# A hybrid encoder kernel: the recurrent mixer's triangular solve in blocks of 8 with Horner steps

## The reference

```python
def rwkv_scan(r, w, k, v, kk, b, reverse):
    def step(state, inp):
        r_t, w_t, k_t, v_t, kk_t, b_t = inp
        sa = jnp.einsum('bhvk,bhk->bhv', state, -kk_t)
        state = (state * w_t[:, :, None, :] + sa[..., None] * b_t[:, :, None, :]
                 + v_t[..., None] * k_t[:, :, None, :])
        return state, jnp.einsum('bhvk,bhk->bhv', state, r_t)
...
    for d in range(2):
        w_log = -jax.nn.softplus(-(w0[d] + jnp.tanh(z @ w1[d]) @ w2[d])) - 0.5
        decay = heads(jnp.exp(-jnp.exp(w_log.astype(f32))))
        a = jax.nn.sigmoid(a0[d] + (z @ a1[d]) @ a2[d])
        kd = heads(k * (1.0 + (a - 1.0) * k_a))
        ys.append(rwkv_scan(rh, decay, kd, vh, kk, kk * heads(a), reverse=(d == 1)))
```

## Time and profile before

| | |
|---|---|
| time, median of 3 runs | 3765.77 us (3765.65 to 3765.84) |
| profiled execution | 3762.42 us, span 3760.6 us |
| mean granted clock of PE | 0.994 of 2.4 GHz |
| PE matmul busy | 3675.8 us, 98% |
| PE weight loads busy | 3401.5 us, 90% |
| DVE busy | 2378.3 us, 63% |
| ACT busy | 424.9 us, 11% |
| recurrent mixer's groups, first layer | 347.3 to 541.0 us |

### The profile page before, as it was taken

One profiled execution on the slowest core, in us unless ns is written; L12 is line 12 of the kernel. 1 busy time (PEld: TensorE's weight loads), 2 busy tenths in 40 slices (PEclk: granted clock), 3 DMA queues, 4 the chain that ended last, 5 costly groups with the idle time before them and its releaser, 6 DMA issues. The chain is left out here.

```text
span 3760.6 us, 63506 instructions
## 1 busy us (share of the span) xinstructions
PE 3675.8 (98%) x26848; PEld 3401.5 (90%) x26848; DVE 2378.3 (63%) x4235; ACT 424.9 (11%) x1010; POOL 1169.8 (31%) x926
## 2 busy tenths in 40 slices
PE   7999999999999999999989999999999999999998
PEld 6778885999999999999977888859999999999998
DVE  7986853894688654444389867539946885444442
ACT  1014211100111000000010232111101110000000
POOL 3610000033333355554245100001333334554552
PEclk9999999999999999999999999999999999999999
DMA  5440113599999999999653401146999999999995
GB/s 167 143 136 23 35 58 118 203 398 409 392 388 405 378 364 362 361 358 371 227 158 123 133 29 35 53 127 226 393 413 385 394 408 380 373 369 359 353 364 205
DMA packets 312536, 994.17 MB, mean 264 GB/s; under 512 B 59341, under 2 KB 170317, under 8 KB 231053
## 3 DMA queue, kind: packets, MB, share of 16 engines
q0 software_dynamic: 118944, 587.71, 40.5%
q1 hardware_dynamic: 193312, 402.41, 29.1%
HBM read 1071.38 MB, written 2.10 MB: 285 GB/s over the span
## 5 line engine op out<-in xcount | busy, mean ns | idle before, releaser
L1840 PE MATMUL bank<-ycT,ex_tile 128*128 128x160 f32 x8192 | 1130.5, 299 | 0.0
L1840 PEld LDWEIGHTS bank<-ycT,ex_tile 128*128 128x128 f32 x8192 | 1115.8, 190 | 7.0 <-issue 6.7
L1913 PEld LDWEIGHTS bank<-ex_W,ex_tile 128*128 128x128 f32 x8192 | 1113.3, 190 | 6.8 <-issue 6.7
L1913 PE MATMUL bank<-ex_W,ex_tile 128*128 128x160 f32 x8192 | 1116.6, 299 | 0.0
L1779 POOL DMA_INDIRECT ex_row<-in_peer_u,ex_rows x244 | 256.8, 1052 | 1529.3 <-DVE ex_rows L2073 1062.1
L2115 DVE CUSTOM_DVE_ANT_0 ex_row<-ex_row,ex_h_wide 128x2048 f32<-128x2048 f32 x192 | 439.1, 2290 | 355.3 <-DMA ex_row<-in_peer_u,ex_rows 353.9
L2121 DVE SCALAR_TENSOR_TENSOR ex_sums<-ex_row,ex_weight,ex_sums 128x2048 f32<-128x2048 f32 x186 | 437.3, 2351 | 349.7 <-DMA ex_row<-in_peer_v,ex_rows 349.4
L1790 POOL DMA_INDIRECT ex_tile<-in_peer_v,ex_wanted x256 | 314.1, 1227 | 486.6 <-PE bank L1913 435.7
L459 PE MATMUL pj_bank<-pj_hT,pj_piece 128*128 128x256 f32 x2048 | 454.6, 382 | 4.4 <-DVE pj_hT L813 4.4
L459 PEld LDWEIGHTS pj_bank<-pj_hT,pj_piece 128*128 128x128 f32 x2048 | 387.3, 190 | 70.2 <-issue 13.7
L1779 POOL DMA_INDIRECT ex_row<-in_peer_v,ex_rows x128 | 125.6, 981 | 247.7 <-DVE ex_sums L2121 187.8
(11 more groups left out here) (395 smaller groups left out, 3460.9 us busy)
## 6 DMA issues: line engine op xcount, KB each, us to landing
ex_tile<-in_peer_uT SPq DMA_DIRECT2D x256, 1024.0 KB, 8.1
pj_piece<-in_w_in SPq DMA_DIRECT2D x32, 2048.0 KB, 8.5
arena<-in_w_out SPq DMA_DIRECT2D x20, 1024.0 KB, 5.1
query_w<-in_peer_w_query SPq DMA_DIRECT2D x16, 1024.0 KB, 6.0
rw_low_rank<-in_w_out SPq DMA_DIRECT2D x12, 512.0 KB, 4.1
ex_row<-in_peer_u,ex_rows POOLq DMA_INDIRECT x314, 9.6
ex_row<-in_peer_v,ex_rows POOLq DMA_INDIRECT x256, 8.8
ex_tile<-in_peer_v,ex_wanted POOLq DMA_INDIRECT x256, 7.9
```

Of the source, the lines that this page charges most:

```text
L1840: mm = mmul(o, ring[:, j % SLOTS, k * P:k * P + P], hT[k // 4][:, k % 4, 0:DENSE], start=(k == 0), stop=(k == KT - 1))
L1913: mm = mmul(bank[:, at_, lo:lo + DENSE], ring[:, i % SLOTS, m * P:m * P + P], W[:, j, :], start=(j == 0 and m % 3 == 0), stop=(j == TILES ...
```

## The change

The block size of the solve goes from 16 to 8. In blocks of 8, N^8 is zero, so W = (I + N + N^2)(I + N^3 + N^6), which is built in two Horner steps: W3 = I + N + N^2 (`w3`), W6 = W3 + N^3 W3 (`h1`), W = W3 + N^3 W6 (`h2`). The part outside the blocks now has four block rows in a chunk, so that (W No)^4 is zero: with M = W No and X0 = W R, R = X0 + M (X0 + M (X0 + M X0)), three Horner steps (`y1`, `y2`, `y3`), each a product and an add on DVE. Nine products a direction stand where eleven stood. The filler in the solve is cut in two halves. `prepare_decays` is split: the scans stay early, and the reciprocal with the four small copies becomes `prepare_inverse`, which follows the last add of the solve. Token shifts and the key square are spread between the steps.

```diff
-    mats["N4T"], mats["N4"], mats["N8"] = mats["NT"], mats["N"], mats["N2T"]
-    Yo = mats["N2"]
+    mats["W6"], mats["W"], mats["MT"] = mats["NT"], mats["N"], mats["N2T"]
+    mats["X0"], mats["X1"], mats["X2"] = mats["Aak"], mats["N3"], mats["W3"]
...
                 for d in range(2):
                     dve(f"nn{d}")
-                    product(d, 2 + 2 * d, mats["N"], mats["NT"])
-                    ev(product(d, 3 + 2 * d, mats["NT"], mats["N"]))
+                    ev(product(d, 2 + 2 * d, mats["N"], mats["NT"]))
                 act("trA")
                 turn("trB", 7, lambda d, b: BTc[:, d, b * P:b * P + P])
                 for d in range(2):
-                    act(f"sq2{d}")
-                    product(d, 2 * d, mats["N2"], mats["N2T"])
-                    ev(product(d, 2 * d + 1, mats["N2T"], mats["N2"]))
+                    act(f"n2{d}")
+                    ev(product(d, 3 + 2 * d, mats["N2T"], mats["N"]))
...
                 for d in range(2):
-                    ev(product(d, 4 + d, mats["N2"], mats["W"]))
-                fill(3 * i)
+                    act(f"n3{d}")
+                    dve(f"w3{d}")
+                    ev(product(d, 2 + 2 * d, mats["N3"], mats["W3"]))
+                fill(3 * i, [0])
                 for d in range(2):
-                    act(f"sq4{d}")
-                    dve(f"w2{d}")
-                    ev(product(d, d, mats["N4"], mats["W"]))
+                    dve(f"h1{d}")
+                    ev(product(d, 3 + 2 * d, mats["N3"], mats["W6"]))
...
+                fill(3 * i, [1])
                 for d in range(2):
-                    ev(product(d, 2 + d, mats["N4T"], mats["N4"]))
+                    dve(f"h2{d}")
+                    ev(product(d, d, mats["W"], R))
+                    ev(product(d, 2 + 2 * d, mats["No"], mats["W"]))
                 for d in range(2):
-                    act(f"sq8{d}")
-                    dve(f"w4{d}")
-                    ev(product(d, 4 + d, mats["N8"], mats["W"]))
+                    act(f"m{d}")
+                    ev(product(d, 3 + 2 * d, mats["MT"], mats["X0"]))
                 for d in range(2):
-                    dve(f"w8{d}")
-                    ev(product(d, d, mats["W"], R))
+                    dve(f"y1{d}")
+                    ev(product(d, d, mats["MT"], mats["X1"]))
                 for d in range(2):
-                    act(f"x{d}")
-                    ev(product(d, 2 + d, mats["NTo"], R))
-                for d in range(2):
-                    act(f"no{d}")
-                    ev(product(d, 4 + d, mats["W"], Yo))
+                    dve(f"y2{d}")
+                    ev(product(d, 2 + 2 * d, mats["MT"], mats["X2"]))
...
                         masked(d, b0, 1, "Rb", "m32" + w + "i", wait=False)
-                        masked(d, b0, 0, "NT", "m16" + w, wait=False)
-                        masked(d, b0, 0, "NTo", "mX" + w, dve_ev)
+                        masked(d, b0, 0, "NT", "m8" + w, dve_ev)
...
-                    do(V.tensor_tensor(eb(mats["N"], d), src, m4("m16" + "LU"[d]), ALU.mult), dve_ev, wait=(d == 1))
+                    do(V.tensor_tensor(eb(mats["N"], d), src, m4("m8" + "LU"[d]), ALU.mult), wait=False)
+                    do(V.tensor_tensor(eb(mats["No"], d), src, m4("mX" + "LU"[d]), ALU.mult), dve_ev, wait=(d == 1))
...
-                grow("w2")
-                grow("w4")
-                grow("w8")
+                    shift(sv[:], 2, i + 1)
+                add("h2", (3, 5), mats["W"], mats["W3"])
                 if i % 2:
                     add_unit((1, 4)[i // 2])
                 if more:
                     prepare_3(i + 1)
-                for d in range(2):
-                    pe(f"z{d}")
-                    do(V.tensor_tensor(jk(R, d), bank[:, 4 + d, :], jk(R, d), ALU.add), dve_ev, wait=False)
+                add("y1", (3, 5), mats["X1"], mats["X0"])
+                add("y2", (0, 1), mats["X2"], mats["X0"])
+                add("y3", (2, 4), R, mats["X0"])
                 if more:
+                    prepare_inverse(nc, do, first)
                     prepare_pairs(nc, do, first, i + 1)
```

More of the change, by code:

```diff
@@ L279, in prepare_decays @@
 def prepare_decays(nc, do, first, i):
[L281 to L282 removed]
+    V, dec, D1, Pc = nc.vector, decay(first, i), first["D1"], first["Pc"]
     for d in range(2):
@@ L1145, in head_sums, with fill @@
                 mmul(bank[:, 7, 0:SEQ], c("heads"), kq[:], start=True, stop=True).then_inc(kq_mm, 1)
-            def fill(m):
+            def fill(m, blocks=range(TB)):
                 u, br = divmod(m, 2)
[L1150 to L1153, removed]
+                if blocks[0] == 0:
+                    pe.wait_ge(chunk_in[m % 4], 16 * (m // 4 + 1))
+                    if m >= 2 and br == 0:
+                        pe.wait_ge(unit_added, u)
+                for b in blocks:
                     for k in range(GT):
@@ L1369, in _ @@
                 for d in range(2):
-                    pe(f"sq2{d}")
-                    do(A.copy(jk(mats["N2T"], d), bank[:, 2 + 2 * d, :]), wait=False)
-                    do(A.copy(jk(mats["N2"], d), bank[:, 3 + 2 * d, :]), act_ev, wait=False)
+                    pe(f"n2{d}")
+                    do(A.copy(jk(mats["N2T"], d), bank[:, 2 + 2 * d, :]), act_ev, wait=False)
                 pe("trB")
@@ L1375, in _ @@
                 for d in range(2):
-                    pe(f"sq4{d}")
-                    do(A.copy(jk(mats["N4T"], d), bank[:, 2 * d, :]), wait=False)
-                    do(A.copy(jk(mats["N4"], d), bank[:, 2 * d + 1, :]), act_ev, wait=False)
+                    pe(f"n3{d}")
+                    do(A.copy(jk(mats["N3"], d), bank[:, 3 + 2 * d, :]), act_ev, wait=False)
                 pe("trK")
@@ L1382, in _ @@
                     kk_root(i + 1)
-                for name, dst, b0 in (("sq8", mats["N8"], 2), ("x", R, 0), ("no", Yo, 2)):
-                    for d in range(2):
-                        pe(f"{name}{d}")
-                        do(A.copy(jk(dst, d), bank[:, b0 + d, :]), act_ev, wait=False)
+                for d in range(2):
+                    pe(f"x{d}")
+                    do(A.copy(jk(mats["X0"], d), bank[:, d, :]), act_ev, wait=False)
+                    pe(f"m{d}")
+                    do(A.copy(jk(mats["MT"], d), bank[:, 2 + 2 * d, :]), act_ev, wait=False)
                 for d in range(2):
@@ L1464, in _, with add @@
                                        pend[:, d, :].unsqueeze(2).to_broadcast([P, NCH, RH]), ALU.mult), wait=(d == 1))
-                def grow(name):
+                def add(name, b0, to, plus):
                     for d in range(2):
                         pe(f"{name}{d}")
-                        do(V.tensor_tensor(jk(mats["W"], d), bank[:, (0 if name == "w4" else 4) + d, :],
-                                           jk(mats["W"], d), ALU.add), dve_ev, wait=False)
+                        do(V.tensor_tensor(jk(to, d), bank[:, b0[d], :], jk(plus, d), ALU.add), dve_ev, wait=False)
                 more = i < GT - 1
-                if not more:
+                for d in range(2):
+                    dve.wait_ge(act_ev, at(ACT_EV, i, f"n2{d}"))
+                    do(V.tensor_tensor(jk(mats["W3"], d), jk(mats["N2T"], d), jk(mats["W3"], d), ALU.add), dve_ev, wait=False)
+                if more:
+                    shift(sr[:], 0, i + 1)
+                    shift(sk[:], 1, i + 1)
+                else:
                     scale_branch(nc, do, col, first, ycT, 2)
                     dve.sem_inc(branch_ready, 1)
+                add("h1", (2, 4), mats["W6"], mats["W3"])
                 if more:
-                    prepare_1(i + 1)
+                    do(V.scalar_tensor_tensor(kq[:], sk[:], col("k_k", i + 1), sk[:], ALU.mult, ALU.mult))
+                    do(V.tensor_scalar(kq[:], kq[:], col("k_k", i + 1), None, ALU.mult), kq_ready)
                     prepare_decays(nc, do, first, i + 1)
-                grow("w2")
-                grow("w4")
-                grow("w8")
+                    shift(sv[:], 2, i + 1)
+                add("h2", (3, 5), mats["W"], mats["W3"])
                 if i % 2:
```

31 lines of the change are left out of this document (16 added, 15 removed).

## The result

The changed kernel takes 3769.84 us (median of 20 runs, 3765.22 to 3773.93), the kernel before 3765.52 us beside it (20 runs, 3757.86 to 3771.12). The ratio is 1.0013 [1.0007, 1.0019]: 4.3 us more, inside 0.2% and inside the stated range, but on the other side of where the forecast of 3757 stood. Nine products for eleven bought nothing as the change stands.

The account below looks back on a forecast made before the run. PE bounds the kernel, DVE close behind, and DVE becomes the bound in groups 0 to 2. Queues -9.6, old half clock -4, new falls +5 give -8.6 us: median 3757, range 3746 to 3771 (own case 3750 to 3763).

Parts of the forecast that it names:

- The wait: Before direction 1's G/H products in groups 0 to 2: PE waits about 4 us, where it was 0.3.
- Four more DVE operations: DVE's queue in each group: ten operations removed, fourteen added, costing 2.6 us more.
- Groups 1 and 2 unchanged by the queues: Groups 1 and 2 of a layer: DVE sets the pace, 43.7 against 44.2 us, length unchanged within 0.5 us.
- Group 3, -4.0: Group 3 of a layer, preparing no next group: PE sets the pace, saved products count in full, -4.0 us.
- Group 0, -0.8 a layer: Group 0 of a layer: products behind the masks come 1.2 us sooner, DVE takes part back, -0.8 us.
- the old falls, -4: Half clock behind group 0's mask waits, both layers: 8.2 us lost in all, half counted as gained, -4 us.
- the price of a fall: Half clock behind each of the six new PE waits: 0.8 us each, +5 us in all.
- The signs: Profile signs: PE wait about 4 us, DVE idle under 3, mask to G add 43 to 44.5, group 3 near 42.4.
- The third: Rival: falls over dense work cost about 2 us each, old ones half kept; -1.6 us, 3764; 27%.
- The fourth: Rival: slower, six falls of 4.5 us each and mask waits keep theirs; +17 us, 3783; 8%.
- The first: Rival: PE stays the bound everywhere, all 28.6 us are gained; 3737 us; 5%.
- The second: Rival: waits come without clock falls, the mask waits' half clock goes too; -17.8 us, 3748; 15%.

Follow-up runs that it names:

- the move alone: Kernel before with only the reciprocal and four small copies put behind the last add of the solve, all eleven products kept: 3801.58 us, ratio 1.0095.
- the kernel whose waits are filled: Changed kernel plus eight unused 256-column matmuls in PE's wait before direction 1's G/H products, groups 0 to 2: 3751.32 us, ratio 0.9970.

## Why the prediction missed

- **The wait came as forecast.** DVE's tail grew, PE's saved 3.6 us a group came back as one wait ahead of direction 1's G/H products in groups 0 to 2: forecast about 4 us, measured 4.02 six times. Its cause is the move (the move alone gives 4.20).
- **Four more DVE operations, 2.6 us.** Right: group 1 has 2.56 us more of DVE (41.86 for 39.30).
- **Groups 1 and 2 unchanged by the queues.** With the clock kept +0.1 and -0.1 us. Right.
- **Group 3, -4.0.** With the clock kept 46.10 for 50.14, -4.0. Right.
- **Group 0, -0.8 a layer, and the old falls, -4.** Together -5.6 forecast for the two layers; measured -3.3 and -4.7, -8.0, since the mask waits' half clock was gone in both layers of the profile. At 3.1 us for 6.8 us of half clock nearly all of this is the clock. The price was sized right there, and that both falls were gone is in part luck of this execution: over all profiles the old solve's two mask waits have half clock behind them in six of six cases, the new solve's one wait in four of fourteen. Profiles of other kernels with the same code at this place have it in one layer and not in the other (43.93 and 47.12 us for group 0 in one profile).
- **The step that failed: the price of a fall, "0.8 each, six of them: +5".** The falls came behind all six waits, as forecast, and cost 2.4 us each, 14.2, by the kernel whose waits are filled. With 14.2 in place of 5 the forecast's own sum is +0.6 us where it was -8.6: no gain. I had taken the first layer's 6.8 us and written that "more than half lies over idle and small products, costs about 1.5", then cut it again for shorter ones. No fall was shorter, and PE is busy 5.93 of the 6.8 us. The rows to see it were at hand: behind the wait come the end of the G/H products and the BH pairs, 2.00 us at full clock, and the first mask of DVE's queue waits for just these pairs. That queue sets the pace of the group, so what the pairs lose is lost. The half clock also began 0.5 to 0.9 us after work came back, not in the wait, so the wait couldn't absorb it.
- **The signs.** Between first mask and G add of group 1 are 45.56 us, with 5.0 of DVE idle, where 43 to 44.5 and under 3 were named; with the clock kept they are 44.31 and 3.7, of which 2.7 are waits and the rest small gaps. DVE's busy time there, forecast as 40.6, was 40.57. Group 3 lost 1.9 us, not 4.0. These misses too are the clock's, but for 0.7 us by which the estimate of some 2 for DVE's waits was too small.
- **The rivals.** The third, "about 2 us each", is the one that came closest: -1.6 by its sum, with 3764 us (the median lies 5.8 above that). With the measured parts: group queues and old falls -15.7, falls +14.2, together -1.5 for the eight groups. The fourth needed 2.9 us a fall, which no fall reached. The first is out. The second describes the kernel whose waits are filled: 14.4 us under before by the medians, where it had 17.8.
- **Still open.** The medians differ by +4.3 us, the groups by -1.5. In the profiles the two state loops have 2.1 us more and the rest of the program 2.2, both in code that is the same. Of the 2.1, 1.8 are one idle time of PE in each loop, in which it waits for nothing that the profile shows (ahead of line 1326, formerly 1320): 0.96 and 0.94 us before, 1.87 and 1.85 after. The kernel with the filled wait took 78.36 and 78.07 us for these loops, as before. I have no cause for it. The changed kernel's profile was also the fastest of its 20 runs, 4.6 us under their median, with a granted clock of 0.991, and others had down to 0.988. Other kernels' profiles have half clock in two more places, at the mask wait of group 0 (3.1 us) and in a state loop (80.5 to 81.7 us for some 78.2, in one of the two loops of five kernels). That the changed kernel's longer runs have these is likely and not shown; the runs of one kernel spread over 9 to 13 us.

The Trainium skill ("TensorE: Matmul & The Clock Gate", Part 1) says that the engine's clock is throttled by default and that activity releases the throttle. By that rule filling the wait should keep the clock up, and the trace agrees: 0.50 granted behind the wait without the eight matmuls, and 1.00 with them, there and through group 1.

The Trainium skill ("Perfetto Trace Analysis", Identifying the Most-Contended Engine) says to optimize the engine with the highest occupancy first. That PE's saving would then count in full was my inference, which the queue sum contradicted; the trace bears out the queue sum, since groups 1 and 2 kept their length with the clock kept.

## What to carry to other kernels

Where a change lightens one engine and lengthens another's queue, ask what then stands last in that queue and who waits for it: here the G add stood behind work for the next group that nobody needed yet, and putting it first was worth 20 us on the changed kernel. A wait of TensorE that a change creates can have a second price, the half clock behind it; read what stands behind the wait, and if the engine that sets the pace waits for exactly that, count most of the time that the doubled durations add: here 2.4 of the 3.0 us that half of 5.93 busy us would be. Where the order can't remove the wait, work that is thrown away (8 matmuls, 3.7 us of PE) can pay: 18.5 us here.

## What the runs showed of the hardware

The counts are over all ten profiles of this case.

- Single waits of 4.0 to 4.2 us ahead of the G/H products had half clock with them each time (twelve of twelve in two profiles), for 6.8 or 10.2 us. It began 0.5 to 1.1 us after work came back in ten of them, and 1.8 to 2.0 us before in two; the waits of 3.9 us inside the solve had it each time too (six of six), from 0.1 to 1.7 us before work came back.
- Shorter waits of the same length had it in some cases and not in others: 1.85 us with 0.99 soon after it in five of six (3.4 us, once 6.8), 1.85 us alone in eight of twelve (3.4 us each), and the single mask wait of 1.21 us in four of fourteen (6.8 us). The pair of 1.39 and 1.21 us in the old solve had it in six of six.
- What a fall costs differs by place: 2.1 to 2.75 us for 6.8 us ahead of G/H products and pairs, 3.1 at the masks, 1.7 for 3.4 us ahead of the pairs, and 0.1 (3.4 us) to 2.1 (6.8 us) ahead of 128-row products of the solve, where part of it lay over the wait.
- GpSimd does a 128 x 512 float32 multiplication in 1042 ns where DVE needs some 690, and DVE's own operations became no slower (masks 684 ns with it and without, adds into the arena 687 and 688).
